# Split products for the linear layers of both layers, and dense weights laid out by the host as one stream of tiles

## What is computed

```python
def hybrid_mixer(xn, w_in, ...):
    z = xn @ w_in                                    # 1024 -> 2368 columns
    a_val, a_gate, b_gate, c_gate, b_in, c_z = jnp.split(z, splits, axis=-1)
    ya = a_val * jax.nn.sigmoid(a_gate)
    ya = causal_depthwise_conv(ya, conv_a_w) + conv_a_b      # 31 taps, 384 channels
    ya = jax.nn.silu(layernorm(ya, ln_a_g, ln_a_b))
    yb = b_gate * causal_depthwise_conv(c_gate * b_in, conv_b_w)   # 3 taps
    c_u, c_v = jnp.split(jax.nn.gelu(c_z), 2, axis=-1)
    c_v = layernorm(c_v, ln_c_g, ln_c_b)
    yc = chunk_spatial_gate(c_u, c_v, gmlp_ws, gmlp_b)
    y = jnp.concatenate([ya, yb, yc], axis=-1)
    y = rmsnorm(y in groups of 64, mix_out_g)
    return y @ w_mix_out

def memory_cross_attention(xn, memn, w_xq, w_xkv, w_xo):
    q = xn @ w_xq
    k, v = jnp.split(memn @ w_xkv, 2, axis=-1)
    p = jax.nn.softmax(q k^T / 16)
    return (p v) @ w_xo

def swiglu(x, w_gate, w_up, w_down):
    return (jax.nn.silu(x @ w_gate) * (x @ w_up)) @ w_down

for layer in range(2):
    h = h + hybrid_mixer(rmsnorm(h), ...)
    h = h + memory_cross_attention(rmsnorm(h), rmsnorm(mem), ...)
    h = h + (swiglu(rmsnorm(h), ...) if layer == 0 else moe_swiglu(rmsnorm(h), ...))
```

## Time and profile before

| what | us |
|---|---|
| median of 3 runs (lowest, highest) | 2892.71 (2880.12, 2893.2) |
| the profiled execution | 2884.54 |
| its span | 2882.8 |
| PE busy | 2665.8 |
| DVE busy | 1879.1 |
| ACT busy | 1084.4 |
| POOL busy | 247.0 |

### The profile page before, as it was taken

How to read it: one execution, slowest core, us unless ns; L and a number is a source line. 1 busy time by engine, 2 the same in 40 slices (tenths; PEclk the granted TensorE clock), 3 DMA queues, 4 the chain that set the end, 5 groups by cost and what they waited for, 6 DMA issues and landing times.

```text
span 2882.8 us, 31202 instructions
## 1 busy us (share of the span) xinstructions
PE 2665.8 (92%) x11607; PEld 2037.1 (71%) x11607; DVE 1879.1 (65%) x2828; ACT 1084.4 (38%) x1140; POOL 247.0 (9%) x280
## 2 busy tenths in 40 slices
PE   9999999999899999999999999799999897877877
PEld 7768999867778888888888888688788453332332
DVE  5331653631388888897888888246523887888775
ACT  1212332021267768677776866121601111110110
POOL 0000000000000000000000000000001344333331
PEclk9999999999899999999999999799999999899999
DMA  6331654521289999999899998442254999999997
GB/s 236 117 117 44 205 182 150 185 88 59 102 307 334 373 333 357 347 352 350 332 372 333 358 347 294 148 146 74 105 190 154 399 421 421 422 421 422 421 421 320
DMA packets 277347, 775.18 MB, mean 269 GB/s; under 512 B 12661, under 2 KB 52735, under 8 KB 244223
## 3 DMA queue, kind: packets, MB, share of 16 engines
q1 hardware_dynamic: 239648, 503.41, 48.6%
q0 software_dynamic: 36864, 268.45, 22.5%
q10 hardware_dynamic: 735, 1.99, 0.2%
HBM read 772.76 MB, written 1.05 MB: 268 GB/s over the span
## 4 chain that ended last, share of the span: by engine, by line
PE 77%; DMA 14%; DVE 5%; issue 2%; ACT 1%; POOL 0%; DVEq 0%; ACTq 0%; POOLq 0%
DMA dense_weights<-in_peer_rows,work 14%; PE banks L692 13%; PE banks L694 13%; PE banks L693 13%; PE banks L531 13%; PE banks L581 5%; PE banks L1069 3%; PE banks L547 2%; PE banks L655 2%; PE banks L659 2%; PE banks L492 2%; PE banks L1031 1%; PE banks L849 1%; PE banks L778 1%; PE banks L805 1%
## 5 line engine op out<-in xcount | busy, mean ns | idle before, releaser
L1967 DVE TENSOR_TENSOR expert_tiles_low<-expert_tiles,expert_tiles_high 128x2048 fp32r<-128x2048 f32 x336 | 752.9, 2286 | 89.8 <-ACT expert_tiles_high L1485 89.6
L1485 ACT ACTIVATE expert_tiles_high<-expert_tiles 128x2048 fp32r<-128x2048 f32 x336 | 624.8, 1912 | 65.6 <-DMA expert_tiles<-in_moe_w_down 52.6
L1069 PE MATMUL banks<-dense_weights,work 128*128 128x512 f32 x952 | 457.7, 633 | 115.7 <-DVE work L2299 115.5
L1069 PEld LDWEIGHTS banks<-dense_weights,work 128*128 128x128 f32 x952 | 186.0, 201 | 376.2 <-issue 208.9
L692 PE MATMUL banks<-expert_tiles_high,gathered_parts 128*128 128x512 f32 x896 | 355.4, 397 | 2.2 <-DVE gathered_parts L1976 2.2
L694 PE MATMUL banks<-expert_tiles_high,gathered_parts 128*128 128x512 f32 x896 | 350.5, 391 | 0.0
L693 PE MATMUL banks<-expert_tiles_low,gathered_parts 128*128 128x512 f32 x896 | 349.9, 391 | 0.0
L2289 DVE CUSTOM_DVE_ANT_0 dense_weights<-dense_weights,banks 128x1024 f32<-128x1024 f32 x238 | 286.2, 1218 | 85.2 <-DMA dense_weights<-in_peer_rows,work 83.4
L1292 POOL DMA_INDIRECT dense_weights<-in_peer_rows,work x238 | 223.7, 940 | 731.1 <-DVE work L2258 372.4
L1674 ACT ACTIVATE work<-work 128x2 f32<-128x2 f32 x129 | 26.2, 203 | 558.9 <-DVE work L2289 555.6
L692 PEld LDWEIGHTS banks<-expert_tiles_high,gathered_parts 128*128 128x128 f32 x896 | 169.0, 189 | 36.3 <-issue 2.4
(11 more groups left out here) (364 smaller groups left out, 3670.1 us busy)
## 6 DMA issues: line engine op xcount, KB each, us to landing
expert_tiles<-in_moe_w_gate SPq DMA_DIRECT2D x112, 1024.0 KB, 5.1
expert_tiles<-in_moe_w_up SPq DMA_DIRECT2D x112, 1024.0 KB, 5.1
expert_tiles<-in_moe_w_down SPq DMA_DIRECT2D x112, 1024.0 KB, 4.8
dense_weights<-in_w_in SPq DMA_DIRECT2D x12, 2048.0 KB, 9.6
dense_weights<-in_w_xkv SPq DMA_DIRECT2D x8, 2048.0 KB, 7.9
dense_weights<-in_w_in SPq DMA_DIRECT2D x10, 1280.0 KB, 13.9
expert_tiles<-in_ffn_w_gate SPq DMA_DIRECT2D x11, 1024.0 KB, 5.1
expert_tiles<-in_ffn_w_up SPq DMA_DIRECT2D x11, 1024.0 KB, 5.2
```

Of the source, the lines that this page charges most:

```text
L1069: mm = pe.matmul(halves[half], diag[(first + j) % 8], pair_row(first + j)[:, 1, half * 512:(half + 1) * 512], start=False, stop=end and j ...
L1485: act.activation(high_tile(j), raw_tile(j), ACT.Copy).then_inc(g.high, 1)
L1967: dve.tensor_tensor(low_tile(j), raw_tile(j), high_tile(j).bitcast(F32), ALU.subtract).then_inc(g.split, 1)
```

## The change

- All linear layers of both mixers and both attentions are computed as three products of split operands, as the feed-forward part is. The products with the rounded activations come first for all k, those with the low parts of the activations after them (`split_group`).
- Every weight tile that is split is rounded by ACT, in `round_until`, which ACT calls ahead of each wait for a group: two tiles beyond that group. A rounded tile lies in one of three slots (`HIGH_RING`) and needs PE to be done with the third tile before it.
- The low parts of all these tiles, those of the feed-forward part too, are computed by POOL (`low_part`) instead of DVE, in place of the raw tile.
- Activations are rounded by ACT (`round_x`, and the same for y and the attention's output) and their low parts made by DVE (`split_x`).
- On DVE, the normalised memory and its split come ahead of the convolution instead of behind it.
- The host lays all dense weights, those of the second block too, in one array in order of use, in tiles of 128 partitions by up to 2048 numbers, each contiguous. SP loads one tile at a time into a ring of seven (`load`). The second block multiplies 32-bit floats as before, from tiles of 256 columns instead of 512.
- The row buffers of the last stage lie in other slots and join at other counts (`BUF_JOINS`).

The core of the diff:

```diff
-RING = 5
-EXP_RING = 7
-SLOT_F = KT * 512
+RING = 7
+HIGH_RING = 3
+TILE_F = KT * 256
-BUF_JOINS = {11: 2 * TOPK + 4, 12: 2 * TOPK + 5, 13: 4 * TOPK + 4, 14: 4 * TOPK + 5}
+BUF_JOINS = {11 + i: (i + 1) * TOPK + 4 for i in range(4)}
...
+    def split_tile(self, size, split, dmas=1):
+        slot, j = self.tile(dmas), len(self.splits)
+        self.splits.append(len(self.need) - 1)
+        self.sizes.append(size)
+        self.pe.wait_ge(split, j + 1)
+        return slot, j % HIGH_RING
...
+            def split_group(bank, tile, widths, high_x, low_x):
+                high, low = tile
+                for k in range(KT):
+                    for i, m in enumerate(widths):
+                        o, n_ = bank[0:m, i * SEQ:(i + 1) * SEQ], slice(i * P, i * P + m)
+                        pe.matmul(o, high[:, k, n_], high_x(k), start=(k == 0 and i == 0), stop=False)
+                        pe.matmul(o, low[:, k, n_], high_x(k), start=False, stop=False)
+                for k in range(KT):
+                    for i, m in enumerate(widths):
+                        mm = pe.matmul(bank[0:m, i * SEQ:(i + 1) * SEQ], high[:, k, i * P:i * P + m], low_x(k),
+                                       start=False, stop=(k == KT - 1 and i == len(widths) - 1))
+                return mm
...
-                x = normed()
+                x = normed_split()
...
-                pe.wait_ge(y_ready, l + 1)
-                linear(("mix_out", l), "v", 2, lambda k: yF[:, k, :], KT, dmas=4)
...
+                split_linear(("mix_out", l), "v", (y_high, y_low_part))
...
-                linear(("q", l), "a", 2, normed(), KT)
+                split_linear(("q", l), "a", normed_split())
...
-                linear(("xo", l), "v", 2, lambda k: oF[:, k, :], KT)
...
+                split_linear(("xo", l), "v", (o_high, o_low_part))
...
+            def low_part(j):
+                n, size = G.splits[j], G.sizes[j]
+                pool.wait_ge(tiles_rounded, j + 1)
+                pool.tensor_tensor(low_tiles[:, n % RING, 0:size], raw_tiles[:, n % RING, 0:size],
+                                   high_tiles[:, j % HIGH_RING, 0:size].bitcast(F32), ALU.subtract).then_inc(tiles_split, 1)
+            for j in range(len(G.splits)):
+                low_part(j)
...
+            def round_until(count):
+                nonlocal rounded
+                while rounded < min(count, len(G.splits)):
+                    j, n, size = rounded, G.splits[rounded], G.sizes[rounded]
+                    if j >= HIGH_RING:
+                        act.wait_ge(*G.freed[G.splits[j - HIGH_RING]])
+                    act.wait_ge(loads[n % RING], G.need[n])
+                    act.activation(high_tiles[:, j % HIGH_RING, 0:size], raw_tiles[:, n % RING, 0:size], ACT.Copy).then_inc(tiles_rounded, 1)
+                    rounded += 1
+            def round_ahead(key):
+                round_until(G.splits_at[key] + AHEAD)
             def ready(key):
+                round_ahead(key)
                 act.wait_ge(group_done, G.after[key])
...
-                key_value(5, 6, 7)
+                key_value(5)
+                for k in range(KT):
+                    act.wait_ge(y_ready, KT * l + k + 1)
+                    act.activation(x_high[:, k, :], yF[:, k, :], ACT.Copy).then_inc(y_rounded, 1)
+                key_value(6, 7)
...
+            def split_x():
+                n = seen.next("xs") - 1
+                for k in range(KT):
+                    dve.wait_ge(x_rounded, KT * n + k + 1)
+                    dve.tensor_tensor(x_low[:, k, :], xF[:, k, :], x_high[:, k, :].bitcast(F32), ALU.subtract).then_inc(x_split, 1)
...
+                if l == 0:
+                    memory()
+                dve.wait_ge(mem_normed, 1)
+                for k in range(KT):
+                    step.then(dve.tensor_scalar(mem_g[:, k, :], mem_hat[:, k, :], c_vec(l, MEM_G, k), None, ALU.mult))
+                step.settle()
+                step.now(dve.tensor_copy(mem_high, mem_g))
+                dve.tensor_tensor(mem_low, mem_g, mem_high.bitcast(F32), ALU.subtract).then_inc(mem_ready, 1)
...
-                dve.wait_ge(ffn_high, j + 1)
-                dve.tensor_tensor(low_tile(j), raw_tile(j), high_tiles[:, j % FFN_HIGH, :].bitcast(F32), ALU.subtract).then_inc(ffn_split, 1)
...
+            load(KT * 16)
+            load(TILE_F, 2 * 4 + 3 + 2 * 4 + 2 + 5 * 4 + 1 + PHEADS)
```

526 lines of the change are left out of this document (247 added, 279 removed).

## The result

| | before | after |
|---|---|---|
| median of the runs, us | 2886.41 (2877.23 to 2893.2) | 2913.84 (2909.25 to 2915.25) |
| the profiled execution, us | 2884.54 | 2913.01 |
| its span | 2882.8 | 2911.3 |
| TensorE's mean granted clock | 0.968 | 0.951 |

After over before is 1.0094, 95% interval 1.0063 to 1.0126: slower by some 27 us. The forecast was 2913.

What follows compares the result with a forecast made beforehand. PE's time per tile was taken as the bound, while the engines preparing tiles keep up. From 2884.5 us, 45 of net gain and 70 of port loss gave 2909, 2913 with half the median's offset; own range 2890 to 2935, whole range 2834 to 2932.

Steps and rivals of the forecast that it cites:

- The alternating price: If POOL and DVE alternate whole instructions in the mixers, their work adds up there: 77 us lost over both layers.
- the taken middle: Port loss of 70 us, between 77 for alternating instructions and 62 for DVE keeping POOL out until the convolution ends.
- the steps: The prediction's own terms laid out by stretch of the span, with 77 us for the port; they sum to +32.
- Rival 2: POOL and DVE share the port finely, each slowed by a part: half of the 70, 2875 us; chance 0.12.
- rival 1: The port costs nothing for these instructions: 2840 us, or 2835 with POOL at its lower bound; chance 0.28.
- the sum of -45: Net effect with the port left aside: 81 us of gain on PE less 36 of new costs.
- PE's gain: In both mixers three split products, 0.356 us, replace one of floats, 0.432; a 256-column tile costs 5.7; 81 us gained.
- The step that counted "0.5 longer" for a norm: Three norms other than the feed-forward part's were each to take 0.5 us longer.
- (a): At the start ACT rounds two weight tiles before squaring x; squares begin near 12.2 instead of 6.4: 7 us lost.
- (b): Before c_var the memory's share stands ahead of DVE's convolution; PE waits some 7 and 2 us, plus 2.3 cold: 11.
- (c): ACT rounds mix_out's first tile only behind y's eight roundings; 7.1 us waiting and 2.3 cold clock per layer: 19.
- (d): The feed-forward part starts some 2.7 us earlier, three other norms take 0.5 longer: -1 in all.

Runs made afterwards that it cites:

- the quarters: The changed kernel with each of GpSimd's subtractions cut into four of a quarter of the columns; 2912.6 us, 1.0102 of before.
- the subtraction of 36.33 us: The changed kernel with GpSimd subtracting 8 columns for tiles 4 to 7 and 9 to 15 of a layer, all columns for tile 8; 2908.63 us.
- the memset kernel: The changed kernel with GpSimd's subtraction replaced by a memset of zeros of the same tile and size; 2844.68 us, 0.9851 of before.

## Why the prediction was right, point by point

**Its mechanism held.** POOL and VectorE hold each other for whole instructions, in the changed kernel in turns. The half that no row of before showed, POOL holding VectorE, is the row of 4860 ns, and with the quarters 1535. The Trainium skill (SBUF — State Buffer, SBUF: two separate sides) has that lock, held for the whole instruction by the one that starts first. The rows agree. By the same section a VectorE instruction with two SBUF inputs collides only with a GpSimd instruction that reads SBUF: the memset's rows agree with that too. By the rule that the one that starts first wins, the subtraction of 36.33 us, shut out by dozens of steps that began after it had asked, would not be there; here the measurement decides.

**The size of the port.** The alternating price was 77 us, the taken middle 70. The kernel with memsets puts it near 62 by the times of the whole, and near 71 by place: against its timeline the changed kernel loses 30 us up to c_var in each layer, and 3 and 8 from there to mix_out, its longer wait for POOL taken off. The 62 are less because the memset kernel in turn loses 5 us in the dense feed-forward part (199.7 for 195.0) and 7 behind the router's sums (2126.1 for 2118.9); its clock is lower in both, and no run looked into why. The prediction by place: 31 us in layer 0 up to c_var, where the stretch grew by 21.5 and the steps gave 21, so that term was sized right; 35 in layer 1, where the steps gave 21 in all and the stretch grew by 14.9. There the scaling of the memory fell into a pause of POOL and took its 2.19 us, as VectorE's rows of the second mixer show; I had counted it as held:

```profile
532.71 2.19 DVE L1791 TENSOR_SCALAR dense_weights<-work,cols 128x256 f32<-128x256 f32 x8
...
549.91 56.41 DVE L1759 SCALAR_TENSOR_TENSOR work<-work,cols 128x256 f32<-128x256 f32 x90
```

Rival 2 is out by the quarters; rival 1 would have been right without the lock, 2840 against the 2844.68 of the memsets. That kernel tests the sum of -45 only in part: it stands 41 us under before, and some 7 of these are the memset's shorter time. So without the port the change is worth 34 to 43 us, for the 45 of the sum, as the port is put at 62 or at 71.

**PE's gain.** Paces as predicted: tiles of the feed-forward part 5.76 us apart, those of mix_out 5.71 for 5.7. What was missed is the clock. The windows around q and around the start of the dense feed-forward part, in the kernel before (the first two) and in the changed one:

```profile
208.00:220.00 12.00, 12.00 (x56) 10.57 (x57) 2.55 (x7) 0.60 (x1) 0.00 (x0) 1.00 0.01 1
287.00:300.00 13.00, 6.60 (x36) 6.29 (x35) 11.80 (x26) 3.67 (x3) 0.00 (x0) 0.74 1.10 351
```

```profile
244.00:256.00 12.00, 11.50 (x83) 11.53 (x84) 5.36 (x15) 7.33 (x11) 6.34 (x2) 0.86 0.25 80
300.00:325.00 25.00, 21.59 (x170) 20.85 (x169) 9.77 (x20) 14.19 (x19) 13.77 (x4) 1.00 0.36 127
```

In the kernel before PE idled for 2.96 us ahead of q, and its granted clock stayed at 1.00. Now it idles for 3.41, half a microsecond more for one rounding, and soon after 15 products are 0.21 apart instead of 0.12, at the lower level: some 1.5 us at q in both layers. The step that counted "0.5 longer" for a norm was right in the wait and wrong in leaving out what follows it. The length of the pause alone doesn't decide it: ahead of the dense feed-forward part PE idles for the same 3.41 us, and its clock stays at 1.00. The lower level stands behind the wait of 35 us too. From c_var to a_mean PE's granted clock is 0.61 in the mean, 0.78 before: the sums of c_var took 3.23 us for 1.65, the mask products 14.5 for 12.7, the transposes 0.7 more, and kv 1 its 1.1. That is 5.2 for the 2.3 that the steps had there.

**(a) the start.** 9.8 for 7. The squares began at 12.7, near the 12.2 of the working. But the 16 sums behind them took 6.69 us where they took 3.71, at the lower level of the clock (0.55 in the mean, 1.00 before) after a wait for them of 6.97 us, 1.02 before; that was left out. Undoing it gave 6.7.

**(b) before c_var, POOL left aside.** 7 us in layer 0 and 2 in layer 1 by its steps; the memset kernel waits 6.48 and 1.82 there. Right.

**(c) mix_out's first tile.** POOL's price for 2048 columns is 4.6 us (4622 ns in the median), over both bounds, 2.2 to 4.4, and the wait was 7.4 in both layers for 7.1 predicted. The Trainium skill (GPSIMD Engine Reference, Performance versus the Vector engine) had 4.5. Without its cause, ScalarE's order, the stretch from c_var to the sums behind mix_out was 7.6 and 6.8 shorter.

**(d)** The feed-forward part's stretch became 5.1 us shorter. Of these 3.0 are the earlier start (2.7 predicted), and 2.1 lie within its 1,584 products (188.1 for 190.2 us): before, the first 22 ran at the lower level of the clock behind a wait of 6.40 us, 0.224 apart; now they run 0.119 apart from the start, the pace of the other 1,562. The prediction had read the 22 slow products and didn't ask whether the shorter wait would spare them. This isn't safe: the memset kernel has the same wait of 3.41 us, and a clock of 0.90 over the next 29 us. And 5.4 us came back behind the router's sums, 3.7 of it between the first sums behind the experts (1813.04 before, 1845.83 after) and the next ones (1826.04, 1855.15). Before, those first sums were broken by 2.77 us in which PE waited for nothing that the trace shows; the gap is gone. Why, no run looked into: it stays open.

**In sum** the overestimates, layer 1 (6), the 5.4 at the end and the feed-forward part's 2, stand against start 3, c_var to mix_out 4 and mix_out to the next sums 3: 32 - 13 + 10 = 29. The forecast of 2913 was nearer than its terms were: that it lies within 1 us is luck. Its sign was hardly more than even on record, 0.41 for slower against 0.36 for faster; what the runs bear out is the mechanism, and the price of the port to within 15 us.

## What to carry to other kernels

Before work goes to GpSimd, look at what VectorE does at that time with its inputs in SBUF, and at who waits for it; a sum kept in a free PSUM bank takes VectorE out of the way at no cost in its own time. Cutting GpSimd's instruction into quarters didn't help (1.2 us), and making it short didn't keep it from waiting: a long row of VectorE steps shut out even 8 columns until its end. And ask of each wait that an edit adds whether TensorE's clock survives it.
